# Hybrid decoder layer: one GpSimd sum per weight pair, six slots of split weights, a fourth pair by seven products, and two-bank VectorE operations

## What is computed

```python
h = rmsnorm(x, g_ffn_pre[l])
ff = (jax.nn.silu(h @ w_gate[l]) * (h @ w_up[l])) @ w_down[l]
x = x + rmsnorm(ff, g_ffn_post[l])
```

## Time and profile before

| what | value |
|---|---|
| median of three runs | 1206.5 us |
| profiled execution | 1206.21 us, its span 1204.5 us |
| granted TensorE clock, mean | 0.998 |
| TensorE busy (matmuls) | 1191.2 us, 99% |
| VectorE busy | 936.3 us, 78% |
| ScalarE busy | 678.0 us, 56% |
| GpSimd busy | 214.4 us, 18% |
| HBM read / written | 227.88 MB / 2.11 MB |

### The profile page before, as it was taken

The page is one execution under the profiler, slowest core; times in us unless marked ns, Lnnn a source line. Parts: engine busy times, 40 slices in busy tenths (PEclk is TensorE's granted clock), DMA queues, the critical chain, the costliest instruction groups (busy, mean ns, idle before and its releaser), DMA issues.

```text
span 1204.5 us, 16367 instructions
## 1 busy us (share of the span) xinstructions
PE 1191.2 (99%) x5760; PEld 998.0 (83%) x5760; DVE 936.3 (78%) x1230; ACT 678.0 (56%) x896; POOL 214.4 (18%) x158
## 2 busy tenths in 40 slices
PE   8999999999999999999999999999999999999997
PEld 7888888888888888888888888888888878888885
DVE  6657877877777755777888888788888788879887
ACT  5654676475554645655556555555655555556553
POOL 1000200000000000004323333422433123313320
PEclk9999999999999999999999999999999999999999
DMA  8657867767686565454665556566456665554552
GB/s 316 208 151 159 227 174 168 177 133 214 165 198 190 189 206 181 169 187 163 210 210 196 183 184 233 181 206 211 165 186 208 231 218 203 196 201 165 206 197 97
DMA packets 122723, 230.67 MB, mean 192 GB/s; under 512 B 8104, under 2 KB 24752, under 8 KB 122032
## 3 DMA queue, kind: packets, MB, share of 16 engines
q1 hardware_dynamic: 122208, 226.85, 60.9%
q0 software_dynamic: 464, 3.15, 0.6%
HBM read 227.88 MB, written 2.11 MB: 191 GB/s over the span
## 4 chain that ended last, share of the span: by engine, by line
PE 94%; DVE 3%; ACT 1%; DMA 1%; issue 0%; POOL 0%; SPq 0%; DVEq 0%; ACTq 0%
PE bank L1713 93%; PE bank L1990 1%; DMA resid<-in_x 1%; DVE w_lo L1068 1%; DVE gT L1282 0%; PE bank L1718 0%; PE bank L1907 0%; ACT w_hi L657 0%; DVE gT L1278 0%; DVE h L1095 0%; DVE w_lo L1554 0%; DVE pre L1260 0%; DVE resid L1706 0%; ACT w_hi L977 0%; DVE pre L1255 0%
## 5 line engine op out<-in xcount | busy, mean ns | idle before, releaser
L1713 PE MATMUL bank<-w_hi,h2T 128*128 128x512 f32 x1126 | 359.3, 390 | 0.0
L1068 DVE TENSOR_TENSOR w_lo<-raw,w_hi 128x1024 fp32r<-128x1024 f32 x172 | 209.3, 1224 | 119.8 <-ACT w_hi L657 119.0
L1554 DVE TENSOR_TENSOR w_lo<-raw,w_hi 128x1024 fp32r<-128x1024 f32 (+1 forms) x164 | 215.8, 1320 | 74.0 <-ACT w_hi L977 72.8
L657 ACT ACTIVATE w_hi<-raw 128x1024 fp32r<-128x1024 f32 x172 | 180.8, 1058 | 160.4 <-PE bank L1713 146.1
L1713 PE MATMUL bank<-hT,w_hi 128*128 128x512 f32 x768 | 270.9, 396 | 0.0
L977 ACT ACTIVATE w_hi<-raw 128x1024 fp32r<-128x1024 f32 (+1 forms) x164 | 156.3, 954 | 168.0 <-PE bank L1713 141.9
L1713 PEld LDWEIGHTS bank<-w_hi,h2T 128*128 128x128 f32 x1126 | 211.4, 188 | 44.0
L1713 PE MATMUL bank<-hT,w_lo 128*128 128x256 f32 x768 | 214.6, 279 | 0.0
L1713 PE MATMUL bank<-w_lo,h2T 128*128 128x512 f32 x543 | 211.3, 389 | 0.0
L1551 DVE TENSOR_TENSOR w_lo<-raw,w_hi 128x1024 fp32r<-128x1024 f32 x166 | 197.8, 1223 | 15.9 <-ACT w_hi L966 14.4
L966 ACT ACTIVATE w_hi<-raw 128x1024 fp32r<-128x1024 f32 x166 | 170.0, 1055 | 67.2 <-PE bank L1713 64.9
(11 more groups left out here) (232 smaller groups left out, 1261.9 us busy)
## 6 DMA issues: line engine op xcount, KB each, us to landing
raw<-in_w_in SPq DMA_DIRECT2D x63, 1024.0 KB, 10.8
raw<-in_w_down SPq DMA_DIRECT2D x88, 512.0 KB, 5.2
raw<-in_w_up SPq DMA_DIRECT2D x80, 512.0 KB, 4.0
raw<-in_w_gate SPq DMA_DIRECT2D x80, 512.0 KB, 4.8
raw<-in_w_out SPq DMA_DIRECT2D x16, 1024.0 KB, 5.1
raw<-in_w_gate SPq DMA_DIRECT2D x4, 1024.0 KB, 5.2
raw<-in_w_up SPq DMA_DIRECT2D x4, 1024.0 KB, 5.8
resid<-in_x SPq DMA_DIRECT2D x2, 1024.0 KB, 7.1
```

The source lines that it names most:

```text
L657: act.activation(part_of(w_hi, rnd, s), src, ACT.Copy).then_inc(hi_done, 1)
L1068: dve.tensor_tensor(part_of(w_lo, rnd, s), raw_sub(rnd, s)[1], part_of(w_hi, rnd, s).bitcast(F32), ALU.subtract).then_inc(lo_done, 1)
L1554: dve.tensor_tensor(slot_blocks(w_lo, slot, piece), seven_blocks(piece, q), slot_blocks(w_hi, slot, piece).bitcast(F32), ALU.subtract)\
L1713: return pe.matmul(out_, lhsT, rhs, start=start, stop=stop, skip_group_check=True)
```

## The change

It does six things in the FFN:

- FULL becomes RRSSRSSR: four S units of eight, 24 pieces; FINAL becomes RRSSRRRR, still two S units. The block sums of the tokens are made for four units (`seven_sums`, `s_fourth`).
- GpSimd makes only t3 (`up_sum_of`). The two sums that follow from t2 become one VectorE operation of 128x2x512, behind the second piece's low part in `unit_lo`.
- GpSimd's t3 is paced in the loop: for the first S unit it waits for the low part of the group's first piece, for the second S unit for the third piece's, for the third S unit for the first S unit's VectorE sum, for the fourth S unit for all pieces of the second S unit. In the down halves it is not paced.
- The ring of slots becomes six: `more_hi` and `more_lo` lie where `resid` was.
- `resid` is written to DRAM (`resid_rows`) before group 1 is loaded, and read back once all but the last 8 pieces are multiplied; the last 8 pieces use four slots.
- In `partial_sums` the last two additions, in `up_sums` and `gate_sums` both token tiles, and in `turned_lo` both banks become one operation each.

The core of the diff:

```diff
-SEVEN = (2, 4, 6)
+SEVEN = (2, 3, 5, 6)
+FF_SLOTS = 6
+END_SUBS = 8
...
-FULL = Plan("RRSRSRSR")
-FINAL = Plan("RRSRSRRR")
+FULL = Plan("RRSSRSSR")
+FINAL = Plan("RRSSRRRR")
...
+            sp.wait_ge(resid_ready, TT * CHUNKS)
+            for t in range(TT):
+                sp.dma_start(resid_rows.ap()[t * P:(t + 1) * P, :], resid[:, t, :]).then_inc(spilled, 16)
...
+            sp.wait_ge(sub_done, N_SUBS - END_SUBS)
+            sp.wait_ge(spilled, 16 * TT)
+            for t in range(TT):
+                sp.dma_start(resid[:, t, :], resid_rows.ap()[t * P:(t + 1) * P, :]).then_inc(resid_back, 16)
...
-            def weight_sums(i, n, plan):
+            def up_sum_of(i, n):
...
                 pool.wait_ge(raw_up[q], up_arrived(i, n))
                 pool.tensor_tensor(b12, b22, b12, ALU.subtract).then_inc(t3_ready, 1)
-                pool.wait_ge(t2_ready, made + 1)
-                pool.tensor_tensor(b22, b22, b11, ALU.subtract).then_inc(t14_ready, 1)
-                pool.wait_ge(lo_done, ff_base(i) + (plan.base[n] + 2))
-                pool.tensor_tensor(b21, b21, b11, ALU.subtract).then_inc(t14_ready, 1)
+
+            def first_pairs_sums(i):
+
+                pool.wait_ge(lo_done, ff_base(i) + 1)
+                up_sum_of(i, SEVEN[0])
+                pool.wait_ge(lo_done, ff_base(i) + 3)
+                up_sum_of(i, SEVEN[1])
 
             with pool.Fori(1, FF_GROUPS - 1) as i:
-                for n in SEVEN:
-                    weight_sums(i, n, FULL)
+                first_pairs_sums(i)
+                pool.wait_ge(t14_ready, sums_index(i, SEVEN[0]) + 1)
+                up_sum_of(i, SEVEN[2])
+                pool.wait_ge(lo_done, ff_base(i) + FULL.base[SEVEN[1] + 1])
+                up_sum_of(i, SEVEN[3])
...
+            def unit_hi(i, odd, plan, m, first=False):
...
+                if first and m >= AHEAD and m < FF_SLOTS:
+                    act.wait_ge(spilled, 16 * TT)
+                act.wait_ge(sub_done, ff_base(i) + (m + 1 - slot_depth(i, m, first)))
...
-                for t in range(TT):
-                    gate_sum_of(i, t, c0)
+                gates = parts(i)[:, 0::2, :]
+                dve.tensor_tensor(gates, gates, bank[:, c0:c0 + 2, :], ALU.add).then_inc(gate_sum, 2)
...
-                for b in range(2):
-                    dve.wait_ge(ff_hi, 2 * i + (b + 1))
...
+                dve.wait_ge(ff_hi, 2 * i + 2)
+                tiles = ffT[:, bass.ds(4 * i, 4), :]
...
+                elif piece == 1:
+                    dve.wait_ge(lo_done, ff_base(i) + (m + 1))
+                    dve.wait_ge(t2_ready, sums_index(i, n) + 1)
+                    pair = raw[:, q, :].rearrange("p (a c) -> p a c", c=512)[:, 1::2, :]
+                    dve.tensor_tensor(pair, pair, raw[:, q, 1024:1536].unsqueeze(1).to_broadcast([P, 2, 512]),
+                                      ALU.subtract).then_inc(t14_ready, 1)
```

More of the change, by code:

```diff
@@ L137, in sums_index, with at_end, ff_slot, slot_depth @@
     if down_half(i) is not None:
-        return 3 * FF_GROUPS - 4 + HALF_SEVEN * down_half(i) + DOWN_SEVEN[down_half(i)].index(n)
-    return 3 * i + (SEVEN.index(n) - 3)
+        return len(SEVEN) * (FF_GROUPS - 2) + 2 + HALF_SEVEN * down_half(i) + DOWN_SEVEN[down_half(i)].index(n)
+    return len(SEVEN) * i + (SEVEN.index(n) - len(SEVEN))
 def sum_banks(odd):
     return (4, 0) if odd else (0, 4)
-def ff_slot(i, odd, m):
+def at_end(i, m):
+    return isinstance(i, int) and i == FF_GROUPS + 1 and m >= DOWN.subs - END_SUBS
+def ff_slot(i, m):
+    if at_end(i, m):
+        return m % AHEAD
     if down_half(i) is not None:
-        return (ff_base(i) + m) % AHEAD
-    return (m + (0 if odd else FULL.subs)) % AHEAD
+        return (ff_base(i) + m - FF_FIRST) % FF_SLOTS
+    return m % FF_SLOTS
+def slot_depth(i, m, first=False):
+    return AHEAD if at_end(i, m) or (first and m < AHEAD) else FF_SLOTS
 def event_of(rnd, unit):
@@ L230, in hybrid_layer @@
         w_lo = sb("w_lo", [P, AHEAD, SUB], F32R)
-        resid = sb("resid", [P, TT, D])
+        resid_home = ExitStack()
+        resid = sb("resid", [P, TT, D], stack=resid_home)
+        resid_home.close()
+        more_hi = sb("more_hi", [P, FF_SLOTS - AHEAD, SUB], F32R)
+        more_lo = sb("more_lo", [P, FF_SLOTS - AHEAD, SUB], F32R)
+        resid_rows = nc.dram_tensor("resid_rows", (SEQ, D), F32)
         columns = sb("columns", [P, 2, P])
@@ L322, in seven_blocks @@
             return (blocks[:, 1:3, :], blocks[:, 3:4, :], blocks[:, 0::2, :], blocks[:, 1::2, :])[piece]
+        hi_slots = [w_hi[:, s, :] for s in range(AHEAD)] + [more_hi[:, s, :] for s in range(FF_SLOTS - AHEAD)]
+        lo_slots = [w_lo[:, s, :] for s in range(AHEAD)] + [more_lo[:, s, :] for s in range(FF_SLOTS - AHEAD)]
+        early_hi_slots = [early[:, 0, s, :] for s in range(AHEAD)]
+        early_lo_slots = [early[:, 1, s, :] for s in range(AHEAD)]
         def slot_blocks(w, slot, piece):
-            return w[:, slot, :].rearrange("p (a c) -> p a c", c=512)[:, 0:1 if piece == 1 else 2, :]
+            return w[slot].rearrange("p (a c) -> p a c", c=512)[:, 0:1 if piece == 1 else 2, :]
         def s_lo12(j):
@@ L639, in _ @@
                 for n in DOWN_SEVEN[half]:
-                    weight_sums(FF_GROUPS + half, n, DOWN_PLANS[half])
+                    up_sum_of(FF_GROUPS + half, n)
         @block.scalar
@@ L990, in ff_group @@
                         first_product(i - 1, FULL, c0)
-                    unit_hi(i, odd, plan, m)
+                    unit_hi(i, odd, plan, m, first)
                     if m == 0 and first:
-                        act.wait_ge(s_summed, 3)
-                        for j in range(3):
+                        act.wait_ge(s_summed, len(SEVEN))
+                        for j in range(len(SEVEN)):
                             act.activation(s_upper(j), s_sum[:, j], ACT.Copy).then_inc(s_rounded, 1)
@@ L1492, in up_sums @@
                 dve.wait_ge(sub_done, ff_base(i) + (subs or plan.subs - 1))
+                if down_half(i) != 1:
+                    ups = parts(i)[:, 1::2, :]
+                    dve.tensor_tensor(ups, ups, bank[:, c0 + 2:c0 + 4, :], ALU.add).then_inc(up_sum, 2)
+                    return
                 for t in range(TT):
@@ L1593, in ff_group @@
                     unit_lo(i, odd, plan, m)
-                    if first and 1 <= m < 4:
+                    if first and 1 <= m <= len(SEVEN):
                         seven_lo(m - 1)
@@ L1757, in wide_columns, with sub_tokens @@
                         after(s)
-            def sub_tokens(count, slot, act_T, pair, k0, last, tiles=range(TT), w_hi=w_hi, w_lo=w_lo):
+            def sub_tokens(count, slot, act_T, pair, k0, last, tiles=range(TT), w_hi=hi_slots, w_lo=lo_slots):
                 pe.wait_ge(lo_done, count)
@@ L1766, in sub_tokens @@
                         lo_x = act_T[:, k, SEQ + t * P:SEQ + (t + 1) * P]
[L1767 to L1769 removed]
+                        mm(bank[:, 2 * pair + t, :], hi_x, w_hi[slot][:, w], k == 0, False)
+                        mm(bank[:, 2 * pair + t, :], hi_x, w_lo[slot][:, w], False, False)
+                        ins = mm(bank[:, 2 * pair + t, :], lo_x, w_hi[slot][:, w], False, k == last)
                 if TT - 1 in tiles:
```

85 lines of the change are left out of this document (43 added, 42 removed).

## The result

The changed kernel takes 1211.69 us (median of five runs, 1211.28 to 1214.35), the kernel before 1206.55 in the same comparison (1206.4 to 1210.08): a ratio of 1.004, 95% interval 1.0029 to 1.0052. It is 0.4% slower. The profiled execution took 1211.28 us, its span 1209.5, against 1206.21 and 1204.5.

A forecast was written before the change was run, and what follows sets the result against it. The prediction took TensorE's matmuls as the bound, other engines counting only where TensorE waits. Loop +2.8, FINAL +0.6 and down projection -1.0 made +2.4 us on 1206.5: 1208.9 us, range 1203.0 to 1213.0.

The forecast's parts named there:

- TensorE's share: Loop: four S units need 180 matmuls, a period of 41.69 us, 0.91 below the measured one, 8.2 us in nine groups.
- VectorE's late stretch: Loop, `turned_lo` to the fourth S unit's third piece: TensorE waits 1.13 us, period 42.91, 0.31 us more per group.
- Together 23.97: Loop: sum of VectorE's work from `turned_lo` to the fourth S unit's third piece, making that piece ready at 26.49 us.
- Rival 3: VectorE's new 2x512 sum is slower than a low part, up to 1.28 us: 1213 us; chance 0.09 with lesser forms.
- GpSimd's sums: Loop: three of four paced sums are hidden; the fourth, beside the R unit's low parts, costs VectorE 1.10 us.
- rival 1: Loop: GpSimd's fourth sum finds a pause and costs VectorE nothing, 42.32 us per group: 1203.6 us; chance 0.24.
- rival 4: Loop: a second GpSimd sum misses its place, 1.10 us more per group: 1219 us; chance 0.05.
- The couples: VectorE: one operation of 1024 for two of 512 saves 0.07 us; only `turned_lo` lies on the late stretch.
- Slots: Ring of six: removes waits of ScalarE for TensorE that weren't on the chain; no gain by themselves.
- FINAL and the down projection: FINAL: second S unit's third piece late, 0.6 us more. Down projection: 1.0 us gained, bounds 0 and 2.2.
- this goes: Down projection: GpSimd's hold on VectorE's low parts, with TensorE standing 0.57 us, disappears with one GpSimd sum per unit.
- rival 2: VectorE makes up its lead and TensorE never stands, -8.2 and -1.0 us: 1197.3 us; chance 0.04.

The follow-up runs named there:

- version without the two delays: The changed kernel with the fourth S unit's t3 on VectorE and `turned_hi` and `turned_lo` one piece later in the groups: 1200.09 us, ratio 0.9944.
- run with three pairs: The changed kernel with the earlier unit order (RRSRSRSR, RRSRSRRR), three S units per FULL group, four slots and GpSimd's first three sums: 1204.85 us.
- other couples undone: The changed kernel with `partial_sums`' last two additions, `up_sums` and `gate_sums` as two operations of 512 each again, `turned_lo` still one: 1211.77 us.
- down half shifted: The changed kernel with the fourth t3 on VectorE and `turned_hi`/`turned_lo` one piece later, also in the first down half: 1200.6 us, repeated 1200.58 us.

## Why the prediction was right, and what was mis-sized

The forecast said 1208.9 us in a range of 1203.0 to 1213.0, and slower as the likeliest. The time came out 2.8 us above it and inside the range, and the mechanism is the one described. Its main term, the loop, was forecast at 2.8 us and measured 5.45. The errors in the other stages (+0.57, -0.21 and -0.41) cancel by chance, so the total is off by what the loop is off.

1. **TensorE's share came and was overdrawn.** The 27 matmuls went; nothing of the 8.2 us arrived. In the version without the two delays the period is 42.00, so 0.60 of the 0.91 per group arrives, 0.68 in the eight groups behind group 1.
2. **VectorE's late stretch**: right in place and cause, undersized. Forecast 42.91, measured 43.18 in this group (717.17 to 760.35). Piece by piece:

| from, to | forecast | measured |
|---|---|---|
| transposes to `turned_lo` | 2.52 | 719.62 - 717.17 = 2.45 |
| to the R unit | 3.39 + 6.15 = 9.54 | 729.25 - 719.62 = 9.63 |
| R unit with GpSimd's sum | 2.26 + 1.10 = 3.36 | 732.63 - 729.25 = 3.38 |
| third S unit | 6.15 | 738.85 - 732.63 = 6.22 |
| fourth, to TensorE's start | 4.92 | 743.85 - 738.85 = 5.00 |
| to the next transposes | 0.09 + 72 x 0.2267 = 16.41 | 760.35 - 743.85 = 16.50 |

The terms make 42.90 against 43.18. None is off by more than 0.1. The first came out shorter, by 0.07; what was mis-sized is the step "Together 23.97" and the one behind it, whose small terms all came out longer, by 0.35 together. An S unit is 6.22, not 6.15: its last two low parts take 2.41 to the next operation in place of 2.26, so the wait for ScalarE's rounding is 0.15 where the forecast had 0.08. From the low part's start to TensorE's matmul are 1.27, not 1.22, so the handover costs 0.05 and stood at nothing; the restart is 0.34 - 0.23 = 0.11, not 0.09. Nine groups make 5.45 of what was forecast as 2.8.

3. **The second S unit's pause**: forecast "about half a microsecond", measured 0.75 - 0.23 = 0.52; that of the fourth 0.85 - 0.23 = 0.62.
4. **The new sum of 2x512**: forecast 1.22 long, measured 1.23 at 725.70 and 1.14 to the next operation. Rival 3 falls. Its price was also too high: 1.28 is the length of a row of two sums, and from start to start they take 2 x 0.60 = 1.20, which is 0.07 more than 1.13 and not 0.15.
5. **GpSimd's sums**: three hidden, the fourth 1.10 by the forecast and 1.08 by the run that cut it short. That decides against rival 1. The unpaced run met rival 4's case in group 1 alone, at 0.93. In the other eight groups the price of 1.10 was too high, 0.09, since the third sum was still hidden there and the fourth had cost as much where it was.
6. **The couples**: three of them are hidden, as said, but not worth 0.07 each: undoing them took 0.06 from VectorE's rest, for all three. For `turned_lo` the forecast counted the later start, and the run with two operations confirms it, 0.32. The Trainium skill (VectorE: DVE Perf Modes, The DRAIN you can't avoid) would have made fewer operations worth more; the changed kernel's trace, like the earlier trace rows, speaks against it: t2 starts at 724.37 and lasts 0.69, and the next operation starts at 724.98. The same section of the Trainium skill adds that a next operation which isn't held starts earlier, which the prediction left out.
7. **Slots**: "no gain by themselves" was the step that failed. The sum came out as if it were right, because it let VectorE's stretch run without a wait for ScalarE, and that is what the six slots make true: without them 0.61 per group more. In the kernel before, the waits of ScalarE for TensorE were off the chain because VectorE had rest; the change took the rest away. The run with three pairs fits this: it has four slots, VectorE rests twice in its stretch (0.44 and 1.49 us in the group at 713.72), and TensorE stands nowhere in the loop. Writing the residual away cost nothing, as said: its two reads are issued at 1179.6 and 1180.0, land within 10.4 us, and VectorE first needs it at 1198.44.
8. **FINAL and the down projection**: +0.39 for +0.6, -1.41 for -1.0. In the other runs with the same down projection the last stage is 233.4 to 233.9 in most profiles, so the gain there is 0.4 to 1.4, within the bounds given. Where in these bounds is chance, for GpSimd's sums are not paced there. In the changed kernel the second of them fell mostly in a wait of VectorE, and TensorE's matmuls at the first S unit start 0.76 apart:

```profile
980.26 1.30 POOL L657 TENSOR_TENSOR raw<-raw 128x512 f32<-128x512 f32 x1 [9.44 <-DMA raw<-in_w_down]
...
982.56 0.28 DVE L1703 TENSOR_TENSOR d_sum<-d_sum,d_whole 128x128 f32<-128x128 f32 x1
```

   With the other couples undone it came later after the transposes (4.82 in place of 3.63) and held up VectorE's token sum by 1.1 us; there they start 1.70 apart:

```profile
981.10 2.22 POOL L657 TENSOR_TENSOR raw<-raw 128x512 f32<-128x512 f32 x1 [10.63 <-DMA raw<-in_w_down]
...
982.08 1.39 DVE L1695 TENSOR_TENSOR d_sum<-d_sum,d_whole 128x128 f32<-128x128 f32 x1
```

   So "this goes" in the prediction holds only where the sum happens to miss VectorE's work.

9. **VectorE makes up its lead** (rival 2): no. It still stands before `turned_lo`, 0.64 where 0.8 was said.

## What to carry to other kernels

When an engine loses its last rest, every term on its path counts, also those that were free before: a handover of 0.05 us, a buffer that comes free 0.3 us later, a sum on a third engine that holds it up. Look for what the engine waits for at the start of its busy stretch and put one piece of work in front of that wait; here this gave 0.72 us per group. Price a helper engine's work by what it takes from the busy one: 1.08 us lost to an operation that the busy engine does in 0.6.

## What was not expected of the hardware

GpSimd's sum of 16 columns took 1.14 us, hardly less than the 1.30 that one of 512 takes where it isn't held up. VectorE's low part had begun 0.16 earlier and lasts about 1.2, so the likely reading is that GpSimd's time was mostly a wait for that operation. No run has the short sum with VectorE at rest, so a fixed cost of about 1.1 us is not excluded. That GpSimd's "busy" time in a timeline holds such waits is seen at the sum of 512, which took 2.21 beside the same low parts. The Trainium skill (SBUF — State Buffer, SBUF: two separate sides) says that of a GpSimd operation and a VectorE operation with two SBUF inputs, whichever starts first locks the port that the two share for its whole instruction; the 2.21 us of the fourth sum and the low parts' 3.46 in place of 2.38 agree.

The time before group 1 is not steady: its transposes came at 543.7 to 544.3 us in eleven of the fourteen profiles, at 545.04 with `turned_lo` as two, and at 545.46 and 547.84 in the two with the down half shifted, though no edit touched the mixer. A single wait of 3.05 us in the mixer made most of the last one. Times of this kernel that lie 2 us apart are told apart by the stage that differs, not by the span.
